# Attention softmax scaling and a head's constants, keys and values: moved from VectorE to ScalarE in the mixer of a hybrid decoder layer

## What is computed

```
s = q k^T / 8, masked                       m = max(max(s), sink)
p = exp(s - m)                              denom = sum(p) + exp(sink - m)
o = (p / denom) v
```

## Time and profile before

| | us |
|---|---|
| median of 3 runs (lowest, highest) | 1380.65 (1379.69, 1382.17) |
| the profiled execution, its own time | 1378.75 |
| span of its profile | 1376.8 |
| TensorE busy | 1300.5 (94% of the span) |
| VectorE busy | 649.2 (47%) |
| ScalarE busy | 365.4 (27%) |
| GpSimd busy | 320.3 (23%) |
| mixer, first product to last | 78.1 to 629.7 |

### The profile page before, as it was taken

The page is one execution under the profiler, slowest core; times in us unless marked ns, Lnnn a source line. Parts: engine busy times, 40 slices in busy tenths (PEclk is TensorE's granted clock), DMA queues, the critical chain, the costliest instruction groups (busy, mean ns, idle before and its releaser), DMA issues. The chain is left out here.

```text
span 1376.8 us, 18077 instructions
## 1 busy us (share of the span) xinstructions
PE 1300.5 (94%) x6552; PEld 796.2 (58%) x6552; DVE 649.2 (47%) x1067; ACT 365.4 (27%) x863; POOL 320.3 (23%) x351
## 2 busy tenths in 40 slices
PE   7999989889988999999999999999999999999993
PEld 6788878788878887995445454333333333333321
DVE  4245989798969898973122214212112211211214
ACT  3023434344333435331110133111111111111112
POOL 2256655556454646120100000000000000000002
PEclk9999999999999999999999999999999999999997
DMA  6722211112121212333226533599999999999975
GB/s 218 248 92 77 78 56 53 55 55 62 46 63 47 62 46 63 110 105 112 76 77 229 208 113 122 221 414 420 419 420 420 421 421 420 421 421 420 420 286 206
DMA packets 165332, 282.92 MB, mean 205 GB/s; under 512 B 5929, under 2 KB 108558, under 8 KB 164494
## 3 DMA queue, kind: packets, MB, share of 16 engines
q1 hardware_dynamic: 156928, 265.83, 51.1%
q10 hardware_dynamic: 7181, 11.90, 2.4%
q0 software_dynamic: 1152, 4.19, 0.9%
HBM read 267.22 MB, written 14.68 MB: 205 GB/s over the span
## 5 line engine op out<-in xcount | busy, mean ns | idle before, releaser
L1904 DVE TENSOR_SCALAR ee<-ee 128x256 f32<-128x256 f32 x32 | 9.4, 294 | 365.8 <-ACT ee L1849 365.8
L2075 POOL DMA_INDIRECT weights_0lo<-expert_out,row x4 | 4.4, 1095 | 491.4 <-issue 491.4
L1674 PE MATMUL bank<-kv_rows,select 128*64 128x512 f32 x512 | 116.9, 598 | 0.8 <-DVE select L1667 0.8
L693 PE MATMUL bank<-h_sums,ring 128*128 128x256 f32 x384 | 95.5, 394 | 0.0
L693 PEld LDWEIGHTS bank<-h_sums,ring 128*128 128x128 f32 x384 | 74.5, 197 | 10.2
L1674 PEld LDWEIGHTS bank<-kv_rows,select 128*64 128x64 f32 x512 | 33.9, 136 | 61.8 <-issue 59.9
L693 PE MATMUL bank<-h_mix,weights_0lo 128*128 128x256 f32 x256 | 61.8, 396 | 6.9 <-issue 5.5
L759 PE MATMUL bank<-rr 128*128 128x64 f32 x448 | 53.8, 272 | 9.8 <-DVE aa L1123 9.8
L693 PE MATMUL bank<-h_sums,weights_0hi 128*128 128x256 f32 x256 | 61.2, 382 | 0.0
L693 PEld LDWEIGHTS bank<-h_mix,weights_0lo 128*128 128x128 f32 x256 | 49.8, 198 | 17.7 <-issue 11.0
L872 ACT ACTIVATE ring<-bank 128x256 f32<-128x256 f32 x72 | 27.4, 381 | 121.3 <-PE bank L693 121.3
(11 more groups left out here) (351 smaller groups left out, 2444.0 us busy)
## 6 DMA issues: line engine op xcount, KB each, us to landing
weights_0lo<-in_w_gate_up SPq DMA_DIRECT2D x11, 2048.0 KB, 16.6
weights_0hi<-in_w_gate_up SPq DMA_DIRECT2D x11, 2048.0 KB, 21.1
weights_0down<-in_w_down SPq DMA_DIRECT2D x11, 2048.0 KB, 19.6
weights_1down<-in_w_down SPq DMA_DIRECT2D x11, 2048.0 KB, 20.5
weights_1lo<-in_w_gate_up SPq DMA_DIRECT2D x11, 2048.0 KB, 17.3
weights_1hi<-in_w_gate_up SPq DMA_DIRECT2D x11, 2048.0 KB, 21.7
weights_2lo<-in_w_gate_up SPq DMA_DIRECT2D x10, 2048.0 KB, 16.9
ring<-in_w_gate_up SPq DMA_DIRECT2D x10, 2048.0 KB, 21.4
```

The lines of the kernel that those rows point to most:

```text
L693: mm = pe.matmul(bank[:, 0:HALF_T], w[:, k], h[:, k], start=(fresh and k == 0), stop=(k == HALF_K - 1), skip_group_check=True)
L1674: mm = pe.matmul(bank[half * SLOTS:(half + 1) * SLOTS, :], sel[q][:, t], h_rows[:, t, half * 512:(half + 1) * 512], start=(t == 0), stop=( ...
L1904: st.link(dve.tensor_scalar(ee[q][:], ee[q][:], BIG, 1.0, ALU.min, ALU.add))
L2075: pool.indirect_dma_start(out=y[:, t, :], out_offset=None, in_=table, in_offset=bass.IndirectOffsetOnAxis(ap=row[:, t:t + 1], axis=0)).the ...
```

## The change

The scaling of the probabilities goes to ScalarE as eight activations (Copy with a per-partition scale from `den`), in two calls of `scaled`, four for each head of the pair. VectorE keeps the sum and the reciprocal and then signals `den_set`. ScalarE also makes the copies `now`, `kcur` and `vcur`, with immediate scale, after `probs_out(2, 3)`; the first ones at the start of turn 0. Decay 2 and decay 3 move up in ScalarE's order, decay 4 comes after read 6 in place of before it. TensorE waits for three scaled tiles ahead of `transposes(0, 4)`, for five ahead of `transposes(4, 8)`, and for eight ahead of `transposes(8, 12)`.

```diff
-            PROJ, MIX, BANKS_READ, Q_READ = 9, 25, 24, 17
+            PROJ, MIX, BANKS_READ, Q_READ = 9, 23, 22, 16
...
# TensorE, piece 3
-                        pe.wait_ge(pn, m + 1)
+                        pe.wait_ge(pn, 8 * m + 3)
                         transposes(0, 4)
+                        pe.wait_ge(pn, 8 * m + 5)
                         transposes(4, 8)
...
# TensorE, piece 4
                         pe.wait_ge(pev, 4 * m + 1)
+                        pe.wait_ge(pn, 8 * m + 8)
                         transposes(8, 12)
...
# ScalarE
+                def head_now(t, par, kv):
+
+                    act.activation(now[par][:], g["pack"][:, t, :], ACT.Copy).then_inc(cur, 1)
+                    act.activation(kcur[par][:], g["k_dup"][:, kv, :], ACT.Copy).then_inc(k_cur, 1)
...
# closing turn
                                               (row_exps, 0, 8), (decay_of, 2, 3)),
-                                              ((decay_of, 4, 5),), ...
+                                              ((scaled, 0), (scaled, 1), (decay_of, 4, 5)), ...
...
+                    if not later(t):
+                        head_now(0, 0, 0)
...
                     for i in range(4):
                         head(row_exps, 2 * i, 2 * i + 2)
+                        if i == 3:
+                            head(decay_of, 2)
                         read(t, par, 1, i)
+                    head(decay_of, 3)
                     if later(t):
                         act.wait_ge(e_used, 4 * t - 2)
                     gate(t, par, 0, 1, e1, None)
-                    head(decay_of, 2)
                     read(t, par, 1, 4)
-                    head(decay_of, 3)
+                    head(scaled, 0)
                     read(t, par, 1, 5)
+                    head(scaled, 1)
+                    read(t, par, 1, 6)
                     head(decay_of, 4)
-                    read(t, par, 1, 6)
...
                     head(probs_out, 2, 3)
+                    act.activation(vcur[par][:], g["v_kv"][:, :, bass.ds(kv * HD, HD)], ACT.Copy).then_inc(v_cur, 1)
+                    if not (isinstance(t, int) and t == NJ - 1):
+                        head_now(t + 1, 1 - par, kvn)
...
+                def scaled(m, mp, u):
+                    if u == 0:
+                        act.wait_ge(den_set, m + 1)
+                    for n in range(NT):
+                        w = slice(P if n == 0 else 0, 2 * P)
+                        act.activation(sc[:, u, n, w], sc[:, u, n, w], ACT.Copy, scale=den[:, u, n:n + 1]).then_inc(pn, 1)
...
# VectorE
-                    if isinstance(t, int) and t == 0:
-                        head_now(0, 0, 0)
...
-                    order.wait()
-                    dve.tensor_scalar(vcur[par][:], g["v_kv"][:, :, bass.ds(kv * HD, HD)], 1.0, None,
-                                      ALU.mult).then_inc(v_cur, 1)
-                    if not (isinstance(t, int) and t == NJ - 1):
-                        if m is not None:
-                            dve.wait_ge(exps, 5 * t)
-                        head_now(t + 1, 1 - par, kvn)
...
-                        k.link(dve.reciprocal(den[:], den[:]))
-                        k.did(dve.tensor_tensor(sc[:, :, 0, P:], sc[:, :, 0, P:],
-                                                den[:, :, 0:1].broadcast_to([P, 2, P]), ALU.mult))
-                        for u in range(2):
-                            last = dve.tensor_tensor(sc[:, u, 1:], sc[:, u, 1:],
-                                                     den[:, u, 1:].unsqueeze(2).broadcast_to([P, 3, 2 * P]), ALU.mult)
-                        last.then_inc(pn, 1)
-                        order.ended(pn, m + 1)
+                        dve.reciprocal(den[:], den[:]).then_inc(den_set, 1)
+                        order.ended(den_set, m + 1)
```

More of the change, by code:

```diff
@@ L494, in mixer_phase @@
             items, taken, sums, joined = sem("items_done"), sem("items_taken"), sem("weight_sums"), sem("quarters_joined")
-            v_ready, qkb = sem("v_ready"), sem("q_k_decay_ready")
+            v_ready, qkb, den_set = sem("v_ready"), sem("q_k_decay_ready"), sem("den_set")
             mem_back, k_back = sem("mem_back"), sem("k_mem_back")
@@ L899, in turn @@
                             for what, *a in ((((decayed_rows,),), ((sink_exp,), (row_exps, 0, 8), (decay_of, 2, 3)),
-                                              ((decay_of, 4, 5),), ((state_rows,), (decay_of, 6, 7), (probs_out, 0, 1)), (),
+                                              ((scaled, 0), (scaled, 1), (decay_of, 4, 5)), ((state_rows,), (decay_of, 6, 7), (probs_out, 0, 1)), (),
                                               ((probs_out, 2, 3),), ((normed,),))[q]):
@@ L999, in _ @@
                 order = Order(dve)
-                def head_now(t, par, kv):
-                    dve.tensor_scalar(now[par][:], g["pack"][:, t, :], 1.0, None, ALU.mult).then_inc(cur, 1)
-                    dve.tensor_scalar(kcur[par][:], g["k_dup"][:, kv, :], 1.0, None, ALU.mult).then_inc(k_cur, 1)
                 def turn(t, par, m, kv, kvn):
```

## The result

The changed kernel takes 1361.45 us (median of 4 runs, 1359.46 to 1362.34) against 1380.89 us for the kernel before beside it. The ratio is 0.9853, with a 95% interval from 0.9841 to 0.9865: it is faster by 19.4 us. Forecast were 1364.8 us (15.8 us faster) with a range from 1359 to 1373. Its profiled execution took 1361.83 us with a span of 1359.9 us.

What follows compares the result with a forecast made beforehand. TensorE was taken to bound the mixer, losing time where it waits for VectorE's program. Turn gains 5.8 + 2.2 + 7.3 + 0.45 = 15.8 us off 1378.75 give 1362.9, plus 1.9 for the median: 1364.8 us, range 1359 to 1373.

Steps and rivals of the forecast that it cites:

- the second chain: VectorE's own program of a turn, unpaused from mask to last addition; reciprocal to `queries` was to shrink to 6.5 us.
- A new wait for decay 4 in front of `mulq(3)`: VectorE was to wait some 2.5 us there, as ScalarE's decay 4 ends 4.4 us after the reciprocal.
- The scaling's price: On ScalarE, 0.29 us at 128 columns and 0.40 us at 256; 2.98 us for eight, bounds 2.1 and 3.8 us.
- rival 4: Slower than before: each scaling on ScalarE costs 0.8 us (0.50 plus 0.3 drain); 1390 us, chance 0.04.
- two waits of 0.6 and 0.45 us: TensorE at the probability transposes waits in two parts; levels 0 and 1 start 0.45 us earlier.
- The slow products behind level 6: TensorE in turns 3, 4 and 5: a product slowed by lower clock after the wait, priced at 1.4 us each.
- Rival 1: The slow products stay in turns 3 to 5 though the level-6 wait goes: gain 12.7 us, 1368.0 us, chance 0.24.
- The term that was mis-sized: VectorE's `mulq(3)` after the move, taken at 2.0 us, with bounds of 0.84 to 3.0 us.
- 0.75 us of slack: Turn 4: L824 starts 0.75 us later than VectorE's additions allow; added to 1.45 us for a gain of 2.2.
- Rival 3: More clock returns, as at the loop's return between turns 4 and 5, or scalings take 2.1 us: 1360 us, chance 0.11.
- The copies on ScalarE cost nothing: Three copies, about 0.4 + 0.2 + 0.6 us, fit ScalarE's 2.86 us idle time behind `probs_out(2, 3)`.
- The gain passes through to the end: What follows the mixer is released by TensorE's own progress and moves forward with it, keeping the 15.8 us.

## Why the prediction was right

- *VectorE's program is the second chain, and the stretch from the reciprocal to `queries` sets the gain.* Right: the late decay 4, which leaves the scalings, the copies and the waits at L768 as they were, takes 15 of the 19 us back.
- *A new wait for decay 4 in front of `mulq(3)`.* Forecast 2.5 us, measured 2.53 to 2.78; decay 4 was forecast to end 4.4 us after the reciprocal, and L1114 starts 4.3 and 4.4 us after it. The 0.1 us counted for the signal to ScalarE is 0.04 us here (209.32 to 209.36).
- *The scaling's price.* Forecast 0.29 and 0.40 us from start to start; eight take 3.0 us as forecast: from the first scaling of a call to the read behind it 1.50 and 1.49 us in turn 2. The price of rival 4, 0.3 us of drain on top of each 0.50, appears in no run; neighbouring scalings overlap. That is more than VectorE's 2.24 us for the same columns, and the move gained all the same.
- *L768.* Forecast two waits of 0.6 and 0.45 us, measured 0.32 to 0.42 and 0.30; the levels behind start 0.7 to 0.9 us sooner and not 0.45, which is turn 7's gain.
- *The slow products behind level 6 go with the wait.* Right: turns 3 and 5 had a mean clock of 0.97 and have 1.00. Rival 1 fell.
- *The term that was mis-sized is `mulq(3)`,* taken at 2.0 us in all turns. It measured 1.2 us in turns 1, 3 and 5 and 2.3 us in turns 2, 4 and 6. With it the stretch was 5.61 and 6.82 us against 6.5. In turn 1 the head start also cleared the additions at the turn's end (1.37 us for two and 1.36 us for the last before, 0.89 and 0.43 after), and the turn gained 1.7 us more than forecast. The working held GpSimd's position as a bound for one instruction; it is a second chain that meets VectorE at two places of every turn.
- *Turn 4 came near its forecast partly by luck.* Forecast were 1.45 us of VectorE's gain and 0.75 us of slack. The last addition, 0.42 us before, met a weight sum and took 1.51 us, so VectorE gained only 0.5 us up to its end, and the turn 1.2 us up to the recurrence output. The other 1.8 us came at the loop's return, where the forecast had nothing. With the 0.2 us of turn 2 that is 2.0 of the 19.8 us.
- *Rival 3, more clock at the loop's return,* came true in part: the return stayed slow, but in turn 4 less so. Its other part, scalings at 2.1 us, did not. Its 1360 us lie nearer the measured 1361.45 than the forecast of 1364.8 does. There is only one profile of the kernel before; over all profiles here the part with the return takes 14.7 to 18.0 us in turns 2 and 4, so how much of the 1.8 us is the change's stays open.
- *"The copies on ScalarE cost nothing"* was right for ScalarE. What was missed is that taking them from VectorE was worth nothing there: the forecast counted 3.6 us of removed work and then a pause of 2.5 us, without saying that the pause alone would have covered the 1.4 us of copies.
- *The gain passes through to the end* held for the medians; in the profiled execution a clock that fell lower at two places behind the mixer hid 2.9 us of it.

## What to carry to other kernels

When a step is moved to another engine, look for the pause that the move makes on the old one: work that fits into that pause need not be moved, and once the pause is removed it must be. Where VectorE and GpSimd both work from SBUF, read their starts side by side before pricing an instruction: the same multiply cost 0.4 or 1.5 us here by which of them came first. An instruction that others wait for, like a reciprocal of 8 columns, is worth trying earlier in its queue, but together with the pause that it removes: here it made one kernel 15 us faster and another, which had hidden work in that pause, 11 us slower.

## What the runs showed that was not expected

- A 256-column multiply or addition on VectorE with both inputs in SBUF takes 0.41 to 0.43 us alone, mostly 0.7 to 0.95 us next to a GpSimd instruction of 0.6 to 0.8 us, and 1.3 to 1.5 us next to a weight sum of 1.3 to 1.5 us. Holding the GpSimd instruction back turns 1.50 into 0.41 us in the same place.
- Shortening one wait of TensorE in the kernel before by 4.7 us in all (5.5 to 0.8) gave nothing (1.0013); in turn 1 its product behind another wait went from 1.94 to 2.95 us. Waits of 1.3 to 2.1 us were followed by the lower clock in some turns and not in others, and no run here says which.
- The hardware loop's return costs TensorE time of its own. From the recurrence output to the next scores it takes 11.3 to 11.4 us without a return and 14.7 to 18.0 us with one, by the kernel and the turn, with 1.1 to 3.5 us idle in front of 16 products that then take up to 6.8 us and 3.6 to 3.7 us elsewhere in the mixer. It took back 2.5 of the 3.1 us that holding GpSimd had saved.
- The granted clock also fell at the start of the output projection (0.62 in a stretch of 4 us in which TensorE was busy throughout, behind a wait of 3.1 us). With the fall at the first expert it made up some 3 us of the profiled execution, more than holding GpSimd at the turn's end changed the time.
